# Row dots alternate with all searches but the first, in a two-layer decoder with a retrieval expert mixer

## The chip, the cores and the metric

The kernel runs on one core of one Trainium2 chip. The metric is device time in microseconds (us) of one execution. Before the change it was 1746.57 us, the median of 3 runs (1742.76 to 1748.43).

## The reference, cut to what matters

Two layers. Each has a mixer (attention in layer 0, a gated recurrence in layer 1) and then an expert channel mixer ("peer"). For every token and each of 8 heads the expert mixer scores two lists of 128 keys, takes the 16 best of each, adds them to 256 candidates, and keeps the 16 best. Each kept pair (i, j) names one of 16384 experts, with a row of 1024 numbers in table U and one in table V:

```python
sv, si = lax.top_k(s, PEER_TOPK)
cand = (sv[:, :, 0, :, None] + sv[:, :, 1, None, :]).reshape(-1, PEER_HEADS, PEER_TOPK * PEER_TOPK)
cidx = (si[:, :, 0, :, None] * N_KEYS + si[:, :, 1, None, :]).reshape(...)
top_s, top_p = lax.top_k(cand, PEER_TOPK)
eidx = jnp.take_along_axis(cidx, top_p, axis=-1)
g = jax.nn.softmax(top_s, axis=-1)
u = u_tab[eidx]
act = jax.nn.gelu(jnp.einsum('thkd,td->thk', u, xb).astype(jnp.float32))
w = (g * act).astype(xb.dtype)
return jnp.einsum('thk,thkd->td', w, v_tab[eidx])
```

There are 256 tokens and 16 meta tokens, 1024 channels, all in float32. Layer 0 mixes 272 tokens, layer 1 only 256.

## The kernel before, in words

The expert mixer (`peer`, once for each layer) handles its tokens in two ways.

The **dense** tokens, 160 in either layer, are multiplied with the whole of U and then the whole of V. Both tables stream through four buffers (`raw`), 128 tiles of 512 KB each, loaded by the SyncE queue (`load_read`): a buffer is loaded again when TensorE has used its tile. TensorE makes 8 float32 matmuls for a tile, which the trace records as 16. For the 160 tokens, the weights g are spread over the expert grid with one-hot matmuls (`hots` on VectorE, `products` on TensorE, `gate_act` on VectorE), in 20 groups of 8 tokens for each half of the grid. The groups of half 0 go between the last 40 tiles of U, two tiles to a group, those of half 1 between the first 40 tiles of V.

The **gathered** tokens, 112 in layer 0 and 96 in layer 1, only fetch the rows that they need. A "row" n is one gather by GpSimd of 128 U rows (then V rows) of 4 KB each, one for each partition, into one of 8 buffers (`bufs`), 512 KB in all. There are ROWS of them for U and as many for V: 112 + 112 in layer 0, 96 + 96 in layer 1. GpSimd fetches row n when its indices are found and row n - 8 has been used (`rows_taken`). VectorE uses a U row by a `dot` (L1482) with a copy of the tokens (`reps`), and a V row by `add_row` (L1496, L1499), a multiply-add into `reps`. Between the two stands `weigh_rows` (L1488), which waits for `row_gelus`: ScalarE's gelu over all dots (L1413). ScalarE's program has that gelu after its last U tile (`take_act`, L1396).

VectorE's program is written out in one order, and rows are dealt into it by hand. Positions of tiles below are counted in the U table or the V table, from 0 to 127.

1. `find`, the search over the score groups, two at a time: 17 groups in layer 0 (9 searches), 16 in layer 1 (8 searches). The first 7 groups (6 in layer 1) belong to gathered tokens. They come first and give the row indices. After each search with `first >= GG`, five in either layer, 6 dots follow (ROWS_PER_FIND).
2. Gates are shifted for the softmax, then 9 dots, then a wait for ScalarE's exp (L1404), which ScalarE makes after U tile 71. VectorE goes on at L1532.
3. The spread operands (`placed`), then 9 dots. TensorE needs `placed` at U tile 84 (L1633), and VectorE then waits for its result (L1548).
4. For half 0 and then half 1, 20 groups m: 2 rows, `gate_act` (L1307) of group m, `hots` (L1285 to L1292) of group m + 1. TensorE starts `products` (L1272) of a group when its `hots` are made, and V's first product (L1313) waits for all `gate_act` of half 0.
5. What is left: row k of `left` waits for V tile 40 + k * 78 // left.

```python
left = 2 * ROWS - n
for k in range(left):
    tile = NG * 2 + k * (LAST_ROW_TILE - NG * 2) // left
```

6. TensorE sums the gathered tokens' results (the folds, L1669) before V tile 112 (those of copies 0 to 2 in layer 0, 0 and 1 in layer 1) and the last copy before V tile 124. Folds 0 to 2 of layer 0 need 96 of its 112 V rows.

Of the kernel before, what the change touches and what calls it, by code (L numbers as in the profile page):

```python
# [35 lines left out]
PH, NK, TOPK, QH = 8, 128, 16, 128  # L36
# [1107 lines left out]
def peer(nc, ctx, mem, d, layer):  # L1144

    def sem(name):
        return ctx.sem(f"peer{layer}_{name}")
# [7 lines left out]
    GG, COPIES, TB = GH + EXTRA, GB + EXTRA, TD + GB * LANES  # L1155
# [68 lines left out]
    spaced, turned, reps_out = sem("spaced"), sem("turned"), sem("reps_out")  # L1224
# [13 lines left out]
    def copy_of(n):  # L1238

        return n // TOPK % GB if n < GH * TOPK else GB  # L1240
# [16 lines left out]
    def fold_at(b):  # L1257

        bank, at = (TURN_BANK, b) if b < 2 else (0, b - 2)
        _, width = tokens_of(b)  # L1260
        at = at * DC * LANES
        return mem.ps[:, bank, at:at + DC * width].rearrange("p (c t) -> p c t", t=width)
# [61 lines left out]
    with nc.Block() as block:  # L1324
# [94 lines left out]
        def _(dve):  # L1419
# [55 lines left out]
            def wait_row(n):  # L1475
                dve.wait_ge(row_in[n % NBUF], 16 * (n // NBUF + 1))

            def dot(n):

                wait_row(n)  # L1480
                buf = bufs[:, n % NBUF, :]
                dve.tensor_tensor_reduce(buf, buf, reps[:, copy_of(n), :], 1.0, 0.0, ALU.mult, ALU.add,  # L1482
                                         dots[:, n:n + 1]).then_inc(rows_taken, 1)
# [18 lines left out]
            def rows(first, last):  # L1502

                for n in range(first, min(last, 2 * ROWS)):
                    if n == ROWS:
                        weigh_rows()
                    if n < ROWS:
                        dot(n)
                    else:
                        add_row(n)  # L1510
                return min(last, 2 * ROWS)

            n = 0
            for first in range(0, G, 2):
                find(first, min(2, G - first))
                if first >= GG:
                    n = rows(n, n + ROWS_PER_FIND)
            step.wait(1)

# [10 lines left out]
            n = rows(n, n + ROWS_AT_SPREAD)  # L1530
# [12 lines left out]
            n = rows(n, n + ROWS_AT_SPREAD)  # L1543
# [7 lines left out]
            for half in range(2):  # L1551
# [3 lines left out]
                for m in range(NG):  # L1555
                    n = rows(n, n + ROWS_PER_GROUP[half])
# [4 lines left out]
            for k in range(left):  # L1561
                tile = NG * 2 + k * (LAST_ROW_TILE - NG * 2) // left
                dve.wait_ge(st.done, V0 * HALVES + 2 * tile)
                n = rows(n, n + 1)
# [236 lines left out]
```

## Time and profile before

| | |
|---|---|
| median of the runs | 1746.57 us |
| the profiled execution's own time | 1746.25 us |
| its span in the trace | 1744.5 us |
| TensorE matmuls busy | 95% |
| VectorE / GpSimd / ScalarE busy | 66% / 36% / 16% |
| moved by DMA | 533.94 MB, 306 GB/s over the span |
| of it the gathers' queue / the stream's queue | 218.13 MB / 314.90 MB |

The layers' expert mixers fill about 165 to 900 us and 1029 to 1735 us of the span. TensorE is busy nearly everywhere, but its busy time is no measure of how fast it goes through tiles: when a tile's data come late, the gap is short and comes often. So the stages are read by the time for one tile, the DMA rate and the granted clock.

### The profile page before, as it was taken

The page shows a single profiled execution, that of the slowest core. Times are in us where ns is not written, and L with a number is a line of the kernel's source. Part 1 is how long each engine was busy: PE and PEld are TensorE (multiplying, and loading weights), DVE is VectorE, ACT ScalarE, POOL GpSimd, SP SyncE. Part 2 cuts the span into 40 slices and gives each one's busy share as a digit, 9 for nine tenths or more (in the row PEclk, how much of TensorE's full clock was granted, in tenths as well). Part 3 has the DMA queues.
Part 4 walks back from the last instruction along what each step waited for, and adds up shares of the span by engine and source line. Part 5 has one row for each costly group of instructions (what it writes and reads, how often), then busy time and mean ns, then how long its engine had stood idle before and what let it go on. Part 6 is the DMA issues. An engine that isn't in the chain of part 4 may idle for free. (4 is left out here: it accounts for less than half of the span.)

```text
span 1744.5 us, 35217 instructions
## 1 busy us (share of the span) xinstructions
PE 1653.8 (95%) x12806; PEld 1550.5 (89%) x12806; DVE 1147.7 (66%) x2449; ACT 278.8 (16%) x752; POOL 631.6 (36%) x538
## 2 busy tenths in 40 slices
PE   8999999999999999999888999989999999999998
PEld 7858899888999998888778888988899999989897
DVE  4562369984699896545648823999458999944442
ACT  4553221111110000000025621211111100000000
POOL 5614011353244445333416621033433444533310
PEclk9999999999999999999899999999999999999999
DMA  4303477999999999999963235799999999999984
GB/s 155 133 13 102 133 265 270 364 381 366 344 408 403 389 398 408 410 409 410 394 241 112 97 125 178 258 349 354 392 336 354 408 391 395 409 405 403 383 341 157
DMA packets 149917, 533.94 MB, mean 306 GB/s; under 512 B 17617, under 2 KB 20434, under 8 KB 149842
## 3 DMA queue, kind: packets, MB, share of 16 engines
q1 hardware_dynamic: 89938, 314.90, 48.3%
q0 software_dynamic: 59904, 218.13, 32.4%
q8 instruction: 35, 0.57, 0.1%
q14 instruction: 40, 0.33, 0.1%
HBM read 531.92 MB, written 1.05 MB: 306 GB/s over the span
## 5 line engine op out<-in xcount | busy, mean ns | idle before, releaser
L308 PE MATMUL ps<-big,raw 128*128 128x160 f32 (+2 forms) x4608 | 701.3, 311 | 22.7 <-DMA raw<-in_u 16.9
L308 PEld LDWEIGHTS ps<-big,raw 128*128 128x128 f32 x4608 | 656.1, 190 | 55.5 <-issue 20.8
L1313 PE MATMUL ps<-big,raw 128*128 (+1 forms) x4096 | 600.9, 304 | 21.9 <-DMA raw<-in_v_rows 8.7
L1313 PEld LDWEIGHTS ps<-big,raw 128*128 128x128 f32 x4096 | 563.9, 191 | 49.6 <-issue 46.0
L1356 POOL DMA_INDIRECT big<-in_u_rows,big x208 | 252.8, 1215 | 589.4 <-DVE big L1482 414.6
L1499 DVE SCALAR_TENSOR_TENSOR big<-big 128x1024 f32<-128x1024 f32 x201 | 258.1, 1284 | 202.3 <-PE ps L1313 127.5
L1356 POOL DMA_INDIRECT big<-in_v_rows,big x208 | 225.8, 1086 | 314.2 <-DVE big L1499 255.9
L1482 DVE CUSTOM_DVE_ANT_0 big<-big 128x1024 f32<-128x1024 f32 x208 | 244.5, 1224 | 10.1 <-DMA big<-in_u_rows,big 10.1
L265 POOL TENSOR_TENSOR wlo<-raw,whi 128x512 fp32r<-128x512 f32 x98 | 136.6, 1411 | 94.5 <-ACT whi L259 94.1
L1396 ACT ACTIVATE big<-ps 128x160 f32 x256 | 77.6, 303 | 545.4 <-PE ps L308 510.7
L393 ACT ACTIVATE big<-h 128x272 f32<-128x272 f32 (+1 forms) x32 | 12.6, 418 | 585.5 <-DVE h L1573 575.2
L1430 DVE MAX8 big<-big 128x8 f32<-128x128 f32 (+1 forms) x99 | 33.6, 339 | 104.6 <-ACT big L1365 92.6
L292 PE MATMUL ps<-xhi,whi 128*128 128x272 f32 x312 | 88.7, 309 | 11.1 <-DVE xlo L432 9.5
L1292 DVE TENSOR_TENSOR i_gate<-i_hot,g 128x512 bf16<-128x512 bf16 x240 | 87.4, 422 | 0.0
L1307 DVE TENSOR_TENSOR big<-big,ps 128x512 f32<-128x512 f32 x80 | 55.0, 687 | 46.4 <-PE ps L1272 30.0
L293 PE MATMUL ps<-xlo,whi 128*128 128x272 f32 x312 | 85.0, 297 | 0.0
L292 PEld LDWEIGHTS ps<-xhi,whi 128*128 128x128 f32 x312 | 61.7, 198 | 15.2 <-issue 12.3
L1272 PEld LDWEIGHTS ps<-i_gate,j_hot 128*128 128x128 bf16 x1920 | 68.2, 97 | 5.5 <-DVE i_gate L1292 2.3
L1272 PE MATMUL ps<-i_gate,j_hot 128*128 128x64 bf16 x1920 | 71.1, 193 | 1.6 <-DVE i_gate L1292 1.6
L259 ACT CAST whi<-raw 128x512 fp32r<-128x512 f32 x98 | 58.6, 618 | 60.8 <-PE ps L297 50.4
L293 PEld LDWEIGHTS ps<-xlo,whi 128*128 128x128 f32 x312 | 61.8, 198 | 0.3
L1288 DVE TENSOR_TENSOR j_hot<-iota,idx 128x1024 bf16<-128x1024 bf16 x80 | 55.1, 689 | 0.0
(184 smaller groups left out, 1143.1 us busy)
## 6 DMA issues: line engine op xcount, KB each, us to landing
raw<-in_u SPq DMA_DIRECT2D x256, 512.0 KB
raw<-in_v_rows SPq DMA_DIRECT2D x256, 512.0 KB
raw<-in_query SPq DMA_DIRECT2D x32, 512.0 KB, 3.3
raw<-in_lru_w SPq DMA_DIRECT2D x24, 512.0 KB, 3.2
raw<-in_mla_down SPq DMA_DIRECT2D x17, 512.0 KB, 3.4
raw<-in_mla_out SPq DMA_DIRECT2D x8, 512.0 KB, 3.3
big<-in_u_rows,big POOLq DMA_INDIRECT x208
big<-in_v_rows,big POOLq DMA_INDIRECT x208
```

What stands on the lines that cost most here:

```text
L259: act.copy(self.mem.whi[:, q % SLOTS, :], self.mem.raw[:, s, e * HW:(e + 1) * HW]).then_inc(self.hi_ready, 1)
L265: eng.tensor_tensor(self.mem.wlo[:, q % SLOTS, :], self.mem.raw[:, s, e * HW:(e + 1) * HW], self.mem.whi[:, q % SLOTS, :].bitcast(F32), AL ...
L292: pe.matmul(out, w, m.xhi[:, x, 0:self.T], start=(x == 0), stop=False)
L293: pe.matmul(out, w, m.xlo[:, x, 0:self.T], start=False, stop=False)
L308: mm = pe.matmul(out, self.mem.raw[:, s, c * P:(c + 1) * P], x[:, c, :], start=(c == 0), stop=(c == DC - 1))
L1272: mm = pe.matmul(o, mem.j_hot[:, t // 2, :, t % 2], mem.i_gate[:, k, t // 2, :, t % 2], start=(k == 0), stop=(k == PARTS - 1))
L1292: ins = dve.tensor_tensor(mem.i_gate[:, k], mem.i_hot[:, :, :, :], pairs(mem.g[:, k, tok], wide_i), ALU.mult)
L1313: return pe.matmul(accumulator(c), mem.raw[:, s, c * P:(c + 1) * P], act_w[:, i, :], start=start, stop=False, skip_group_check=True)
L1356: pool.indirect_dma_start(bufs[:, b, :], None, (u_rows if n < ROWS else v_rows)[:, :], bass.IndirectOffsetOnAxis(rows_at[:, k:k + 1], 0)). ...
L1396: act.activation(act_w[:, bass.ds((turn - U0) * UNROLL + s, 1), :], mem.ps[:, s % 2, 0:TD].unsqueeze(1), ACT.Gelu_apprx_tanh).then_inc(st. ...
L1482: dve.tensor_tensor_reduce(buf, buf, reps[:, copy_of(n), :], 1.0, 0.0, ALU.mult, ALU.add, dots[:, n:n + 1]).then_inc(rows_taken, 1)
L1499: dve.scalar_tensor_tensor(rep, bufs[:, n % NBUF, :], w, rep, ALU.mult, ALU.add).then_inc(rows_taken, 1)
```

## The change

The condition after a search becomes `if first:`. The dots start after the second search: 8 times 6 in layer 0, 7 times 6 in layer 1. As dots now run before all copies of the tokens must have been made, the first dot of every 16 rows gets a wait for its copy.

```diff
             def dot(n):
 
                 wait_row(n)
+                if n % TOPK == 0:
+                    dve.wait_ge(reps_out, 2 * copy_of(n) + 2)
                 buf = bufs[:, n % NBUF, :]
                 dve.tensor_tensor_reduce(buf, buf, reps[:, copy_of(n), :], 1.0, 0.0, ALU.mult, ALU.add,
                                          dots[:, n:n + 1]).then_inc(rows_taken, 1)
...
             n = 0
             for first in range(0, G, 2):
                 find(first, min(2, G - first))
-                if first >= GG:
+                if first:
                     n = rows(n, n + ROWS_PER_FIND)
             step.wait(1)
```

## Rows read from the trace of the kernel before

**Rows 1.** Windows by stage: window, length, busy time (instructions) by engine, clock, DMA share, GB/s.
```profile
660.50:845.70 185.20, 174.38 (x1157) 158.36 (x1154) 97.94 (x78) 0.00 (x0) 77.07 (x77) 1.00 1.03 409
845.70:890.10 44.40, 36.54 (x242) 35.47 (x241) 25.81 (x22) 0.00 (x0) 14.95 (x13) 0.85 0.97 367
1517.50:1691.60 174.10, 167.01 (x1159) 157.70 (x1155) 77.40 (x62) 0.00 (x0) 57.18 (x58) 1.00 1.01 397
236.70:292.00 55.30, 55.30 (x410) 55.30 (x409) 52.17 (x201) 9.55 (x29) 0.00 (x0) 1.00 0.69 228
292.00:437.40 145.40, 136.42 (x939) 128.17 (x939) 112.35 (x309) 20.67 (x62) 62.10 (x48) 1.00 0.97 367
1137.00:1295.60 158.60, 149.19 (x1040) 141.85 (x1039) 118.04 (x333) 22.79 (x69) 63.85 (x48) 1.00 0.94 355
```

**Rows 2.** TensorE's waits: who waited for whom, us in total, times, longest.
```profile
PE ps L308 <- DMA raw<-in_u: 16.9, 34, 2.2
PE ps L1669 <- DVE big L1499: 6.6, 1, 6.6
```

**Rows 3.** Timeline of TensorE at the folds: start, length, instructions, idle before and releaser.
```profile
845.70 3.65 PE L1669 MATMUL ps<-con,big 128*128 128x32 f32 x32
855.99 3.62 PE L1669 MATMUL ps<-con,big 128*128 128x32 f32 x16 [6.64 <-DVE big L1499]
...
1695.13 26.33 PE L1313 MATMUL ps<-big,raw 128*128 128x160 f32 x192
```

**Rows 4.** Windows behind layer 0's fold (the clock stands before the DMA share).
```profile
856.00:860.00 4.00, 4.00 (x18) 4.00 (x19) 3.26 (x3) 0.00 (x0) 3.08 (x4) 0.50 1.04 410
860.00:865.00 5.00, 5.00 (x24) 5.00 (x23) 4.55 (x4) 0.00 (x0) 2.15 (x3) 0.60 1.00 392
```

**Rows 5.** Timeline of TensorE in layer 0's U tiles, between searches.
```profile
307.55 4.93 PE L308 MATMUL ps<-big,raw 128*128 128x160 f32 x32 [0.16 <-DMA raw<-in_u]
...
369.67 7.49 PE L308 MATMUL ps<-big,raw 128*128 128x160 f32 x48 [0.73 <-DMA raw<-in_u]
```

**Rows 6.** Timeline of VectorE from the searches to the spread, both layers.
```profile
246.19 0.19 DVE L1470 SCALAR_TENSOR_TENSOR big<-big 128x32 uint32<-128x32 f32 x1
...
290.20 1.22 DVE L1482 CUSTOM_DVE_ANT_0 big<-big 128x1024 f32<-128x1024 f32 x1
...
410.72 0.44 DVE L1532 TENSOR_REDUCE big<-big 128x17 f32<-128x272 f32 x1 [14.55 <-ACT big L1404]
...
438.83 0.56 DVE L1548 CAST idx<-ps 128x160 bf16<-128x160 f32 x2 [10.70 <-PE ps L1633]
...
1271.23 0.42 DVE L1532 TENSOR_REDUCE big<-big 128x16 f32<-128x256 f32 x1 [24.82 <-ACT big L1404]
```

**Rows 7.** Timeline of three engines where layer 1 goes from U to V.
```profile
1407.63 0.69 DVE L1307 TENSOR_TENSOR big<-big,ps 128x512 f32<-128x512 f32 x1
...
1410.17 1.23 DVE L1482 CUSTOM_DVE_ANT_0 big<-big 128x1024 f32<-128x1024 f32 x1
1411.28 0.89 PE L1272 MATMUL ps<-i_gate,j_hot 128*128 128x64 bf16 x24
...
1411.32 1.23 DVE L1482 CUSTOM_DVE_ANT_0 big<-big 128x1024 f32<-128x1024 f32 x1
1411.58 0.30 ACT L1396 ACTIVATE big<-ps 128x160 f32 x1 [1.87 <-PE ps L308]
...
1412.46 0.69 DVE L1307 TENSOR_TENSOR big<-big,ps 128x512 f32<-128x512 f32 x1
...
1413.40 3.77 PE L1313 MATMUL ps<-big,raw 128*128 128x160 f32 x26 [1.24 <-DVE big L1307]
```

**Rows 8.** Timeline of layer 0's gelu over dots and the first V rows.
```profile
619.98 0.30 ACT L1413 ACTIVATE big<-big 128x112 f32<-128x112 f32 x1 [66.13 <-DVE big L1482]
...
622.39 0.28 DVE L1488 TENSOR_TENSOR big<-big 128x112 f32<-128x112 f32 x1
...
623.58 1.28 DVE L1499 SCALAR_TENSOR_TENSOR big<-big 128x1024 f32<-128x1024 f32 x1
```

## The prediction

> **What bounds the kernel now.** I read the page's slices first, then TensorE's waits, then windows by stage, then timelines where two stages meet. TensorE is the path to the end, but three different things set its pace.
>
> In the first 25 tiles of layer 0's U table it sets its own pace: 410 matmul records are 25.6 tiles in 55.3 us, 2.16 us a tile, while DMA moves only 228 GB/s [rows 1]. At the end of layer 1, where no row is fetched any more, 12 tiles take 26.33 us, 2.19 us each [rows 3]. That is TensorE's own pace.
>
> From 292 to 437 us, where rows are fetched in bursts between searches, 939 records are 58.7 tiles in 145.4 us: 2.48 us a tile [rows 1]. The reader is to see the waits for in_u in many small pieces, 34 of them, none over 2.2 us [rows 2].
>
> In V behind the groups DMA is full. Layer 0: 72 tiles in 185.2 us, 2.57 us a tile, at 409 GB/s; layer 1: 72 tiles in 174.1 us, 2.42 us, at 397 GB/s [rows 1]. One transfer of 524 KB takes 1.28 us at 409 GB/s, and a tile and a row together 2.56 us. So layer 0's tail goes at one row for each tile, though 96 rows are dealt over 78 tiles (1.23 a tile): rows fall behind, and at the fold TensorE stands 6.64 us for them [rows 3], then works at half clock (0.50 and 0.60, so 1.2 GHz for most of 9 us) [rows 4]. Stretches differ in what a fetched row costs TensorE: nothing to 0.4 us early, and up to 1.28 us in a full tail.
>
> **The change, part by part.** Dots done at the end of the searches go from 30 to 48 in layer 0 and from 30 to 42 in layer 1. All later dealings keep their size, so every later row is 18 (12) earlier in VectorE's order, and `left` shrinks from 96 to 78 in layer 0 and from 64 to 52 in layer 1. The count of dots, gathers and bytes is the same. The first use of a buffer moves from behind the fifth search (dots at 290.20) to behind the second, whose indices are made at 246.19 [rows 6]; GpSimd's gathers follow, as each waits for the row 8 before it.
>
> *VectorE's chain* becomes later by 18 dots of 1.15 us (1410.17 to 1411.32 [rows 7]), 20.7 us, in layer 0 and by 13.8 us in layer 1. It now stands 14.55 and 24.82 us for ScalarE's exp, and in layer 0 again 10.70 us for TensorE's spread result [rows 6]. Layer 1 is covered. In layer 0 6 us are not, but the exp itself comes later by what TensorE loses below, and the second wait hides the rest. Were that cover gone, the price would be the difference, 6 us at most. I take 0.
>
> *The added wait* holds VectorE, and behind it the following searches, until a copy of the tokens is made. ScalarE makes all copies before the scores that the second search waits for, so it is over before it is reached. 0.
>
> *30 gathers move into early U tiles.* Before, three bursts of 6 stand between 307.55 and 369.67: 25 tiles in 62.1 us [rows 5] against 25 x 2.19 = 54.8, so 7.4 us for 18 gathers, 0.41 us each. Over 292 to 437.4: 145.4 - 58.7 x 2.19 = 16.8 us for 48 gathers, 0.35 each; layer 1, 1137 to 1295.6: 158.6 - 65 x 2.19 = 16.3 us for 48, 0.34 each [rows 1]. I take 0.38: +6.8 us in layer 0 (three bursts more), +4.6 us in layer 1 (two more). Bounds: 0, as DMA has 409 - 228 = 181 GB/s spare there [rows 1], and 1.28 each, 38 us, if nothing is spare. The rows nearest are the bursts themselves.
>
> The Trainium skill (DMA: Bandwidth & Descriptors, Queues, rings and completion order) says each DMA engine takes turns between its queue rows packet by packet. Layer 0's tail agrees (one row for one tile at 2.57 us a tile), and it speaks against this change: a burst of gathers takes half of the bandwidth while it lasts, however much is spare on average, and the tail's pace does not rise while a row is due for each tile.
>
> *Layer 0's tail.* 78 rows over 78 tiles is still one row for each tile, so tiles 40 to 110 stay at 2.56 us. Only the last two before the fold are free of gathers: -1 us. Between the bounds 0 and 185.2 - 72 x 2.19 = -27.5 I take this by the pair's own rate.
>
> *Layer 0's fold.* Row 208, the last that folds 0 to 2 need, is now due at tile 102, so the fold at tile 112 waits for nothing, and the last gathers are issued by tile 110. Before, 845.7 to 890.1 took 44.4 us [rows 1]. After: three folds at 3.65 / 2 = 1.83 us [rows 3], 5.5 us, and 12 tiles at 2.19, 26.3 us, together 31.8: -12.6 us. That holds the wait, the half clock and the late gathers.
>
> *Layer 1's tail.* 52 rows over 78 tiles are 0.67 a tile. With the tile that is 1.67 x 1.28 = 2.13 us of DMA for 2.19 us of TensorE: TensorE's pace again, with DMA nearly full. Before, 0.82 a tile made 2.33 us and 2.42 were measured. I take 2.25: 162 us for 174.1, -12 us. Bounds: 0, and 174.1 - 157.7 = -16.4.
>
> *A new wait in layer 1.* U rows there are 96. Before, 48 + 40 dots are done when half 0 of the groups ends, and row 96 comes in half 1. After, 42 + 18 + 2 x 18 = 96: row 96, and with it `weigh_rows`, stands at group 18 of half 0, ahead of `gate_act` of group 18 and `hots` of group 19. It waits for a gelu that ScalarE makes only after the last U tile. It is no deadlock, as TensorE can do both last tiles without `hots` of group 19, but then TensorE stands. By rows: ScalarE takes the last tile from 1411.58 to 1411.88 [rows 7]; gelu 0.30, to 1412.2; weigh and first V row 1.19 (622.39 to 623.58), second 1.28 [rows 8], to 1414.7; gate_act and hots 2.54 (1407.63 to 1410.17), to 1417.2, where products were at 1411.28. Then two more rows, 2.57, to 1419.8, and V starts 0.94 after the gate_act (1412.46 to 1413.40), at 1420.7 for 1413.40 [rows 7]: +7.3 us. TensorE has then stood some 5.8 us, and after 6.64 us it fell to 1.2 GHz, which cost half of 4 us and 2 of the next 5 [rows 3, 4]; part falls in the wait here, so +3.2. Together +10.5. Bounds: 0 if hidden, 14 with twice the clock loss. Layer 0 has 112 U rows: 48 + 18 + 40 = 106, so its row 112 falls into half 1, where the gelu is free. 0.
>
> **The sum.** +6.8 + 4.6 - 1 - 12.6 - 12 + 10.5 = -3.7 us on the profiled execution's own 1746.25: 1742.5. That execution is 0.3 us under the median of the runs, so 1743 against 1746.57.
>
> **The rivals.**
> (A) *Layer 1's new wait doesn't cost.* For it: V behind it waits for data in small pieces (2.42 us a tile against 2.19), and four filled buffers could give some back. Against: the groups' stretch behind it is TensorE's, and its own tail has little left to give. Without +10.5: 1732.
> (B) *Layer 0's tail speeds up.* If arbitration favours the stream once fewer rows are outstanding, tiles go at 2.40, not 2.57: -12 more, 1731. Against: 2.57 us a tile holds for 72 tiles on end.
> (C) *Slower, by the early bursts.* They now start at tile 5, and layer 0 has eight in a row, so buffers never refill. The highest price of a burst is the 0.41; if it is 0.8 for each of 30 gathers, they cost 24 for 11.4, and the sum is +8.9: 1755.5. From 0.68 on the change is slower by the bound below. For it: in 292 to 437 DMA is at 0.97 with only 367 GB/s. Against: two layers give 0.34 and 0.35.
> (D) *Layer 1's tail stays at 2.42 us a tile*, since its irregular dealing, and not bytes, makes its gaps: +12, 1755.
> (E) *The dots don't run early*, since a row or copy is late. The rows were long there when the first dot ran at 290.20 [rows 6]: no wait of VectorE for DMA stands ahead of it. 1746.5.
>
> **How the numbers follow.** About 5 us (0.3%) either way is what runs of this kernel can tell from no change. Forecast 0.50 (own range 1737 to 1750; 0.12 of it below 1741.3, 0.36 same, 0.02 slower), A 0.15, B 0.08, C 0.14, D 0.10, E 0.03. Faster 0.12 + 0.15 + 0.08 = 0.35; same 0.36 + 0.03 and 0.01 of C's near end: 0.40; slower 0.25. Range 1730 to 1757.
>
> **What would show it.** First dot near 246 us, bursts of 6 from 248 on, U tile 84 of layer 0 near 444 instead of 437. No wait of TensorE at layer 0's fold, its clock 1.00 there; 2.56 us a tile before, 2.19 after. In layer 1 weigh_rows (L1488) ahead of the last `products` of half 0, with TensorE idle near 6 us and a clock under 1.00. A tail of layer 1 near 162 us. I am wrong if the early U tiles lose much more or less than 11 us, if the new wait is missing, or if either tail goes at another pace.

## The result

Over 20 executions of each kernel the median went from 1748.60 to 1756.37 us: ratio 1.0048, 95% interval 1.0029 to 1.0067. The change makes the kernel 0.5% slower; 1743 us was forecast for it, with "no change" as the likeliest outcome. One of the changed kernel's 20 executions took 3346.73 us and is not in the ratio.

The profile after needs care. Its execution took 1745.20 us (span 1743.4), the least of the 20 and 1 us less than the profiled execution before. The two spans say nothing about the change; the stages do. Windows of the changed kernel, to be read beside [rows 1] (length, busy time and instructions by engine, clock, DMA share, GB/s):

```profile
663.70:848.10 184.40, 174.52 (x1159) 158.41 (x1155) 92.19 (x73) 0.00 (x0) 71.82 (x72) 1.00 1.03 409
848.10:881.20 33.10, 33.10 (x242) 33.10 (x242) 8.37 (x8) 0.00 (x0) 0.00 (x0) 0.95 0.64 219
1521.20:1690.60 169.40, 162.53 (x1157) 157.26 (x1154) 62.12 (x50) 0.00 (x0) 44.23 (x46) 1.00 0.98 370
232.80:441.40 208.60, 194.75 (x1347) 183.79 (x1346) 185.42 (x545) 30.35 (x91) 81.56 (x66) 1.00 0.95 360
1083.30:1289.70 206.40, 193.84 (x1347) 183.68 (x1346) 171.43 (x508) 30.28 (x91) 77.56 (x60) 1.00 0.94 353
```

The five windows are layer 0's tail and fold, layer 1's tail, and the first 84 U tiles of either layer. Fold of layer 0: 44.4 us became 33.1, with no gather left in it. Tail of layer 0: 184.4 for 185.2, at the same 409 GB/s. Tail of layer 1: 169.4 for 174.1, with 12 gathers less but DMA at 0.98 and only 370 GB/s. The first 84 U tiles, the same 1347 matmul records, take 208.6 and 206.4 us. Over the same tiles the kernel before took 200.7 (236.7 to 437.4) and 200.1 us (1095.5 to 1295.6), with 48 gathers in each for 66 and 60 now. TensorE's waits (us in total, times, longest), beside [rows 2]:

```profile
PE ps L308 <- DMA raw<-in_u: 23.8, 51, 1.6
PE ps L1272 <- DVE i_gate L1292: 6.6, 3, 5.7
```

The wait of the fold (L1669, 6.64 us) is gone; 51 small waits for U tiles stand for 34, and a new one of 5.7 us for `hots`. Here it is, where layer 1 goes from U to V, beside [rows 7] and [rows 8] (timeline):

```profile
1405.38 0.30 ACT L1396 ACTIVATE big<-ps 128x160 f32 x1 [1.87 <-PE ps L308]
1405.58 0.27 ACT L1413 ACTIVATE big<-big 128x96 f32<-128x96 f32 x1
...
1405.88 0.26 DVE L1490 TENSOR_TENSOR big<-big 128x96 f32<-128x96 f32 x1 [7.01 <-ACT big L1413]
1406.18 0.75 DVE L1498 TENSOR_SCALAR big<-big 128x1024 f32<-128x1024 f32 x1
1407.05 1.28 DVE L1501 SCALAR_TENSOR_TENSOR big<-big 128x1024 f32<-128x1024 f32 x1
...
1408.25 0.68 DVE L1307 TENSOR_TENSOR big<-big,ps 128x512 f32<-128x512 f32 x1
...
1410.79 2.67 DVE L1501 SCALAR_TENSOR_TENSOR big<-big 128x1024 f32<-128x1024 f32 x2
1410.93 1.46 PE L1272 MATMUL ps<-i_gate,j_hot 128*128 128x64 bf16 x24 [5.69 <-DVE i_gate L1292]
...
1414.31 1.14 PE L1313 MATMUL ps<-big,raw 128*128 128x160 f32 x3 [1.92 <-DVE big L1307]
```

`weigh_rows` (now L1490) stands 7.01 us for ScalarE's gelu over the dots, which comes only behind the last U tile; the V rows (L1498, L1501), the gate (L1307) and the `hots` queue behind it, and TensorE's `products` wait 5.69 us for those. Behind this idle time the granted clock stands at 0.50, that is 1.2 GHz, for two windows of 5 us:

```profile
1405.00:1410.00 5.00, 0.24 (x2) 0.00 (x0) 3.96 (x7) 1.76 (x3) 1.99 (x2) 0.97 0.63 200
1410.00:1415.00 5.00, 2.15 (x27) 2.03 (x28) 4.90 (x9) 0.00 (x0) 2.53 (x3) 0.50 0.67 206
1415.00:1420.00 5.00, 5.00 (x20) 5.00 (x20) 3.47 (x5) 0.00 (x0) 2.53 (x3) 0.50 0.66 206
```

Why the span hides the loss is outside the changed stages. In attention, where both kernels are the same, the execution before ran a while at half clock and the one after did not (windows of before, then of after):

```profile
130.00:135.00 5.00, 5.00 (x18) 3.88 (x17) 0.00 (x0) 2.79 (x7) 1.41 (x2) 0.50 0.00 0
```
```profile
130.00:135.00 5.00, 5.00 (x37) 4.66 (x37) 0.44 (x1) 3.31 (x6) 3.10 (x4) 1.00 0.02 3
```

Layer 0's U tiles begin 3.9 us earlier after it (232.8 for 236.7), and between the end of layer 0 and layer 1's U tiles, before the first early dot of layer 1, another 3.2 us are gained: 7.1 us that the change didn't bring. That the clock makes most of the 3.9 us fits the other profiles: thirteen (all but e10's) have the same code up to layer 0's U tiles, which begin anywhere from 232.8 to 238.8 us, and in the five with a mean clock of 0.66 from 125 to 140 us they begin at 236.3 us or later.

### The profile page after: what moved, and what is told of

Same layout as the page of the kernel before. It is cut to its first block and busy times, and to the rows that moved or that the text cites. A ratio compares the mean times of both kernels' runs of the same rounds, so it can differ in the third digit from the quotient of the medians.

```text
span 1743.4 us, 35228 instructions
## 1 busy us (share of the span) xinstructions
PE 1649.6 (95%) x12806; PEld 1546.6 (89%) x12806; DVE 1148.1 (66%) x2449; ACT 278.6 (16%) x752; POOL 638.6 (37%) x538
## 5 line engine op out<-in xcount | busy, mean ns | idle before, releaser
L1501 DVE SCALAR_TENSOR_TENSOR big<-big 128x1024 f32<-128x1024 f32 x201 | 257.8, 1283 | 217.1 <-PE ps L1313 191.4
L1356 POOL DMA_INDIRECT big<-in_v_rows,big x208 | 234.6, 1128 | 349.9 <-DVE big L1501 282.0
L393 ACT ACTIVATE big<-h 128x272 f32<-128x272 f32 (+1 forms) x32 | 12.6, 418 | 648.0 <-DVE h L1575 637.8
L1307 DVE TENSOR_TENSOR big<-big,ps 128x512 f32<-128x512 f32 x80 | 54.7, 683 | 43.1 <-PE ps L1272 26.2
```

The lines of the kernel that those rows point to most:

```text
L1356: pool.indirect_dma_start(bufs[:, b, :], None, (u_rows if n < ROWS else v_rows)[:, :], bass.IndirectOffsetOnAxis(rows_at[:, k:k + 1], 0)). ...
L1501: dve.scalar_tensor_tensor(rep, bufs[:, n % NBUF, :], w, rep, ALU.mult, ALU.add).then_inc(rows_taken, 1)
```

## The experiments

Twelve kernels ran, in three groups; in each group the kernel before ran beside them on the same chip, and its medians there are 1738.14 (e0 to e3), 1737.47 (e4, e5, e7, e8) and 1740.11 us (e6, e9, e10, e12). e5, e6, e8, e9 and e10 ran once each, so they are read by their stages alone. Stages are lengths between TensorE's rows in the profiles: "U" is U tiles 0 to 83, "end of U" tiles 84 to 127, "V start" V tiles 0 to 39, "tail" V tiles 40 to 111, "fold" from the first fold (L1669) to the last.

**The change again, whole and by layer.** e0_after_again is the changed kernel unaltered. The other two:

```diff
-                if first:
+                if first >= (2 if layer == 0 else GG):    # e2_layer0_only
+                if first >= (2 if layer == 1 else GG):    # e3_layer1_only
```

> The changed kernel unaltered, once more, to see which of its stages repeat. Theory 1 (the stages of the expert mixers make the change: by the first profile +7.8 early and -11.3 at the fold in layer 0, +6.2, +6.8, +2.8 and -4.7 in layer 1, together about +6 us): those stages repeat within 1.5 us, and the time is 4 to 9 us above the kernel before. Rival (the whole difference is drift between executions, since the first profile of the changed kernel was even 1 us shorter than the one before): the stages spread by more than 3 us and the time is within 3 us of the kernel before.

> Early dots in layer 0 alone, layer 1 as before. Theory 1: layer 0 pays 7.8 us early and gets 0.9 + 0.9 + 11.3 back in its tail and at its fold, so 5 us under the kernel before. Rival (the changes of layer 0 cancel, its fold wait being worth less in most executions than in the one profiled): within 2 us of the kernel before.

> Early dots in layer 1 alone, layer 0 as before. Theory 1: 6.2 + 6.8 + 2.8 - 4.7 = 11 us above the kernel before. The prediction's sizes would give 4.6 + 10.5 - 12 = +3. Rival (cancelling in layer 0, above): about +8, the whole difference.

Measured ratios to the kernel before: e0 1.0059 (1.0040 to 1.0078), +10.2 us; e2 0.9986 (0.9970 to 1.0003), -2.4 us; e3 1.0078 (1.0058 to 1.0098), +13.6 us. The two parts add up to 11.2. The loss is layer 1's. Layer 0's gain is not resolved from none. A layer that a kernel leaves alone serves as another profile of before, so each stage has two profiles unchanged and three changed (means, us):

| stage | layer 0 | | | layer 1 | | |
|---|---|---|---|---|---|---|
| | unchanged | changed | difference | unchanged | changed | difference |
| U | 199.5 | 208.5 | +9.0 | 199.3 | 205.7 | +6.4 |
| end of U | 117.4 | 117.5 | +0.1 | 117.3 | 123.9 | +6.6 |
| V start | 104.4 | 103.9 | -0.5 | 104.0 | 106.6 | +2.6 |
| tail | 185.1 | 184.5 | -0.6 | 174.2 | 171.5 | -2.7 |
| fold | 44.2 | 33.1 | -11.1 | 29.7 | 30.8 | +1.1 |
| sum | | | -3.1 | | | +14.0 |

The sums agree with the measured -2.4 and +13.6 us. Stages with the same code spread by up to 5 us among these five profiles, most in layer 1's tail (169.4, 170.9, 174.2), so a single profile would not have shown this. The later kernels e1, e4, e5, e6, e8 and e9 leave all of layer 0, and the U tiles 0 to 83 of layer 1, as in the changed kernel. With them nine profiles stand for either: layer 0's U is 205.9 us in the mean (202.0 to 209.6) and layer 1's 206.0 (203.8 to 207.4), so +6.4 and +6.7 us against the two unchanged ones. The +9.0 of the table comes from three profiles that happened to be long. e3 also shows the fold wait where layer 0 is unchanged (timeline), so it was no accident of the first profile:

```profile
852.68 3.62 PE L1671 MATMUL ps<-con,big 128*128 128x32 f32 x16 [6.56 <-DVE big L1501]
```

**Layer 1's new wait taken away.** e1_cap_half0:

```diff
-                    n = rows(n, n + ROWS_PER_GROUP[half])
+                    n = rows(n, min(n + ROWS_PER_GROUP[half], ROWS if half == 0 else 2 * ROWS))
```

> Rows of half 0 of the groups stop at the last U row, so that weigh_rows never stands in half 0. Theory 1 (the new wait in layer 1 costs its 7 us and 3 us of half clock): the last 44 U tiles of layer 1 fall from 124.6 to 118 us, the first 40 V tiles from 106.9 to 104, and 4 more rows in the tail cost about 1 us: 8 to 9 us under the changed kernel, 0 to 3 us under the kernel before. Rival (stalls there are given back, as full buffers follow them): under 4 us gained.

Ratio 1.0001 (0.9983 to 1.0019), 10 us under e0 (1.0059). End of U 115.8 us, V start 103.8, no wait at V's first product beyond the usual:

```profile
1402.12 4.58 PE L1313 MATMUL ps<-big,raw 128*128 128x160 f32 x32 [0.98 <-DVE big L1307]
```

So the wait costs what the stages say, and no later stage gives a visible part of it back; its tail, with 56 rows, took 175.9 us. This one wait is the whole difference between the changed kernel and the one before, as far as the interval of about 3 us either way can tell: without it, the rest of the change comes out at nothing.

**How much of it is the clock.** e4_filler is the changed kernel with the last turn of layer 1's U tiles written out:

```diff
+                    if s == GROUPS_AFTER[1]:
+                        keep_busy(pe, mem, TURN_BANK, 44)
                     if s in GROUPS_AFTER:
                         products(pe, 0, NG - 2 + GROUPS_AFTER.index(s))
+                keep_busy(pe, mem, TURN_BANK, 12)
```

> The changed kernel with filler matmuls in layer 1 where TensorE waits (44 before the last products of half 0, 12 behind them), so that it stays active; the waits themselves stay. Theory 1 (the fall to 1.2 GHz is what costs the stage behind the wait its 2.8 us and the products 0.6): granted clock 1.00 there, the first 40 V tiles of layer 1 from 106.5 to 104 us, the last 44 U tiles 123 to 124 us as before, 3 us under the changed kernel. Rival (the slow tiles behind the wait come from late data, not from the clock): 106 us stay.

Ratio 1.0032 (1.0009 to 1.0055), 4.7 us under e0 with intervals that overlap. Timeline and one window:

```profile
1399.15 4.97 PE L202 MATMUL ps<-filler 128*128 128x256 bf16 x44
1405.00 0.90 PE L1272 MATMUL ps<-i_gate,j_hot 128*128 128x64 bf16 x24 [0.89 <-DVE i_gate L1292]
...
1408.38 4.59 PE L1313 MATMUL ps<-big,raw 128*128 128x160 f32 x32 [1.17 <-DVE big L1307]
```
```profile
1410.00:1415.00 5.00, 5.00 (x57) 4.96 (x57) 3.82 (x6) 0.00 (x0) 2.36 (x2) 1.00 0.85 288
```

The clock stays at 1.00 and V start falls to 104.0 us, while the end of U stays at 123.7. So 2.6 us of the two stages' 9.2 are the half clock, the rest is the wait. This rests on the stages; the total alone would not show it.

**What a fetched row costs where DMA has room.** The prediction had layer 1's tail near 162 us. These leave out V rows of layer 1's tail (n is cut at 2 * ROWS - SKIP in GpSimd's and VectorE's loops and in the folds' waits); e9 deals its rows in pairs. A row that is left out is neither fetched by GpSimd nor added by VectorE:

```diff
+    SKIP = 52 if layer == 1 else 0        # e5; 13 in e8, 26 in e6 and e9
-            for n in range(2 * ROWS):
+            for n in range(2 * ROWS - SKIP):
...
+                kk = k - k % 2 if layer == 1 else k        # e9
+                tile = NG * 2 + kk * (LAST_ROW_TILE - NG * 2) // left
```

> The changed kernel without the last 52 V rows of layer 1: they are neither fetched nor added (part of the computation is left out). Its tail (V tiles 40 to 111) is then stream alone. The prediction's threshold and the rival price agree here: 72 tiles at TensorE's own 2.19 us, 158 us, for 169 to 171 with the rows.

> The changed kernel with only 39 of the last 52 V rows of layer 1, dealt evenly, one row every second tile (13 rows are left out of the computation). DMA is asked for 1.5 transfers for each tile, 1.92 us of DMA for 2.19 us of TensorE. Theory T (the prediction's: a row costs nothing while DMA has room): 158 to 160 us for V tiles 40 to 111. Theory P (a fixed price for each row): about 158 + 39 x 0.24 = 167. Theory I (irregular dealing makes the gaps, not the number): 158 to 160, and 26 rows dealt in pairs would be dearer than 26 dealt singly.

> The changed kernel with only 26 of the last 52 V rows of layer 1, one every third tile (26 rows are left out of the computation). So far V tiles 40 to 111 of layer 1 took 156.6 us with no row, 170.2 with 39 and 169.4 to 170.9 with 52. Price for each row (0.35 us): 165 to 167 us. Threshold further down (DMA asked for 1.33 transfers a tile): 157 to 159.

> The same 26 rows, dealt in pairs, two every sixth tile. If a row costs because it lengthens the landing of the three loads under way, two at once lengthen it more but half as often: within 3 us of single dealing. If unevenness is what costs, over 5 us more than single dealing.

| rows in layer 1's tail | 0 | 26 | 26 in pairs | 39 | 52 | 56 | 64 |
|---|---|---|---|---|---|---|---|
| tail, us | 156.6 | 167.6 | 167.2 | 170.2 | 169.4, 170.9, 173.7, 174.2 | 174.1, 175.9 | 174.1, 174.3, 177.6 |
| us a row over 156.6 | | 0.42 | 0.41 | 0.35 | 0.30 | 0.33 | 0.29 |

The columns of 52, 56 and 64 rows hold every profile with that number (173.7 is e4, 174.1 with 56 rows e7, 177.6 e12); the last row goes by their means.

With no rows all of it is one unbroken stretch:

```profile
1520.96 156.74 PE L1314 MATMUL ps<-big,raw 128*128 x1152
```

No threshold shows down to 26 rows: these already cost 11 us, at one third of a row for a tile, and the step from 64 to 52 rows is worth some 3. Regular dealing doesn't help (39 rows) and pairs don't harm. The DMA view (window of 100 us; issues, KB, median us from issue to landing) says why. For e5, e8 and e1 in layer 1's tail, then e0 among the U tiles of layer 1:

```profile
raw<-in_v_rows SPq DMA_DIRECT2D x46, 512.0 KB, 3.7
```
```profile
raw<-in_v_rows SPq DMA_DIRECT2D x42, 512.0 KB, 6.2
big<-in_v_rows,big POOLq DMA_INDIRECT x22, 7.3
```
```profile
raw<-in_v_rows SPq DMA_DIRECT2D x41, 512.0 KB, 6.3
```
```profile
raw<-in_u SPq DMA_DIRECT2D x36, 512.0 KB, 6.6
```

A buffer is reloaded when its tile is used, and it is needed again three tiles later, after 3 x 2.19 = 6.6 us. Alone, loads land in 3.7 us. In e8, with one row for two tiles, a gather takes 7.3 us to land, so one is nearly always under way, and the median load lands in 6.2 us, though DMA carries only 331 GB/s in that window. The traces hold the landings of only some of the loads. The quickest, the median and the slowest of them, for the loads of e5 and then e8 in the same windows, and what TensorE waited for in the whole tail of e8 (in e5's it waited for nothing):

```profile
DMA to landing us min/median/max: 3.1/3.7/4.8
```
```profile
DMA to landing us min/median/max: 3.5/6.2/7.2
```
```profile
PE ps L1314 <- DMA raw<-in_v_rows: 9.0, 11, 1.6
```

So without rows no load comes near 6.6 us, and with them the slowest come after it; the waits that this view counts are 9.0 of the 13.6 us. The pairs of e9 show it tile by tile: every six tiles two gathers go out, and TensorE then does six tiles (96 records) without a break and waits once for a load:

```profile
1555.10 13.30 PE L1314 MATMUL ps<-big,raw 128*128 x96 [0.98 <-DMA raw<-in_v_rows]
1569.53 13.30 PE L1314 MATMUL ps<-big,raw 128*128 x96 [1.13 <-DMA raw<-in_v_rows]
```

The median of its recorded loads is 4.6 us, under the lead: only loads beside a pair come late, and a median doesn't show them. What TensorE waits for is a load each time, never VectorE, so it is the gathers that cost and not the adding that was left out with them.

**The lead made shorter.** e10_short_lead:

```diff
     def load_read(self, sp, turn, s, src):
-        sp.wait_ge(self.done, (turn - 1) * HALVES + 2 * (s + 1))
+        sp.wait_ge(self.done, (turn - 1) * HALVES + 2 * (s + 1) + 1)
```

> The changed kernel with every load of the stream in the expert mixers issued half a tile later (it waits until TensorE has also used the first half of the next tile). Nothing else changes. A buffer is free for 3 tiles (6.6 us at TensorE's pace) before it is needed; the load lands after 3.7 us with no rows and after 6.2 to 6.6 us (median) with rows beside it. Theory L (rows cost by making the landing longer than this lead): with 2.5 tiles, 5.5 us, nothing changes where no rows are fetched (12 tiles behind the fold of layer 1, 29.7 us), while the U tiles between searches and layer 1's tail lose 8 us or more each (layer 0's U stage from 207 to over 215, layer 1's tail from 170 to over 178). Rival (rows cost through the DMA rate alone, which is full at moments): those stages stay within 3 us.

1832.79 us. Windows of layer 0's U tiles and of layer 1's tail, and the 12 tiles behind layer 1's fold on the timeline:

```profile
237.40:462.20 224.80, 195.94 (x1347) 185.39 (x1346) 184.90 (x545) 30.33 (x91) 89.00 (x66) 0.99 0.91 341
1593.50:1777.50 184.00, 165.11 (x1159) 157.47 (x1156) 61.94 (x50) 0.00 (x0) 44.95 (x46) 1.00 0.93 340
```
```profile
1781.02 26.33 PE L1313 MATMUL ps<-big,raw 128*128 128x160 f32 x192
```

Where rows are fetched, the same tiles take 15 us or more longer in layer 0's U (224.8, for 202.0 to 209.6 over nine profiles) and 9 to 14 us longer in layer 1's tail (183.4, as 0.6 of the 184.0 stand before tile 40, for 169.4 to 174.2), while DMA is less busy than in the first profile after (0.91 for 0.95, 0.93 for 0.98). Where none are, nothing changes (26.33 us, as in [rows 3]). What rows cost hangs on the lead of the loads. That more lead, with more than the four buffers, would make rows free was not tried.

**Bursts or single gathers.** e7_spread_dots, on top of e1:

```diff
-                find(first, min(2, G - first))
-                if first:
-                    n = rows(n, n + ROWS_PER_FIND)
+                def one():
+                    nonlocal n
+                    n = rows(n, n + 1)
+                find(first, min(2, G - first), one if first > 2 else None)
+                if first == G - (2 - G % 2):
+                    n = rows(n, n + ROWS_PER_FIND)
```

`find` calls `one` after three of the five steps of each of its two top-16 searches.

> As e1_cap_half0, but the six dots are spread through the next search, one after every second or third step of it, instead of in a row after it, so that gathers leave one by one, about 3.5 us apart. Same rows, same bytes. Theory B (it is the burst that costs, since six gathers in a row take half of the bandwidth for 15 us and three loads ahead can't cover that): the first 84 U tiles fall from 202 to 207 us to under 196 in both layers, so 10 to 20 us under e1_cap_half0. Theory P (every gather delays a tile by 0.35 to 0.5 us wherever it stands): 202 to 207 us stay, time within 3 us of e1_cap_half0.

Ratio 0.9961 (0.9941 to 0.9980); U 205.2 us in layer 0 and 201.1 in layer 1. Layer 1's U is 5 us under the 206.7 of e1 and under all nine profiles with bursts (203.8 or more); layer 0's is 3 us over its 202.1 but inside the stage's spread. Neither theory's number is met: U doesn't fall below 196, and against e1 the kernel gains 7 us by the ratios (0.9961 for 1.0001), with intervals that just miss each other, or 4.6 by the medians, and not the 10 to 20 of theory B nor the 3 at most of theory P. That bursts cost more than single gathers is so in layer 1 and open in layer 0.

**A version from the runs.** e12_more_in_layer0, e7 with:

```diff
-                find(first, min(2, G - first), one if first > 2 else None)
+                find(first, min(2, G - first), one if first > (2 if layer == 0 else GG) else None)
+                if layer == 0 and first:
+                    one()
```

> A version by what the runs show: rows of half 0 stop at the last U row; in layer 0 one dot more at each search (8 more, all spread through the searches), so that its tail gets 72 rows for 78 tiles, under one a tile; in layer 1 the dots start at the old place, but spread through the searches. Expected against e7_spread_dots: layer 0 early +3 us, its tail 184 to about 177 us, layer 1 within 2 us; against the kernel before 0.6% less time (e7 0.4% less). Rival: the tail of layer 0 stays at 184 us, as near the full rate a row fewer buys nothing; then equal to e7 or 3 us slower.

Ratio 0.9917 (0.9888 to 0.9946), median 1725.09 us: it beats both kernels. Windows of layer 0's U tiles and tail, then layer 1's:

```profile
237.70:440.90 203.20, 193.32 (x1347) 183.72 (x1346) 188.09 (x550) 30.24 (x91) 87.14 (x67) 1.00 0.97 372
664.00:845.70 181.70, 171.69 (x1156) 158.08 (x1153) 85.97 (x69) 0.00 (x0) 65.75 (x66) 1.00 1.02 401
1081.30:1276.70 195.40, 189.34 (x1347) 183.25 (x1346) 157.27 (x480) 30.19 (x91) 62.80 (x48) 1.00 0.92 343
1497.60:1675.10 177.50, 168.67 (x1156) 157.81 (x1153) 76.78 (x62) 0.00 (x0) 58.36 (x58) 1.00 1.00 387
```

Layer 0 has 74 dots done before its groups, for 66 in the changed kernel. Its U tiles take 203.2 us, within the 202.0 to 209.6 of the changed kernel's, and its fold takes 33.1 us without a wait. Its tail of 72 rows is 181.7, not the 177 expected. Layer 1 with its 30 dots spread has U at 195.4 for 199.3, but its tail of 64 rows is 177.6 for 174.2. All stages of the table together make -10 us against the unchanged ones, and the profiled execution, 1729.76 us, is 10.4 us under the kernel before. The rest of the 14 us lies between this execution and the median, 4.7 us below it.

## Why the prediction was wrong

- **Layer 1's tail was the step that failed.** The prediction put 52 rows at 2.25 us a tile, 162 us, "TensorE's pace again": -12 us. Measured: 171.5 for 174.2, -2.7 (-2.1 with e4's tail). The rule behind it, that a row costs nothing while DMA has room on average, is false here: 26 rows cost 11 us (e6), and the price is there from the lowest number tried, as it works through the landing time against a lead of three tiles (e5, e8, e10). The prediction's own early rows, 0.34 to 0.41 us each at DMA shares under 1, contradicted the tail's price of near zero (0.06 us a tile over 2.19, so 4 us for 52 rows); it used one price early and another late for the same thing. Its own check of the rule on the tail before had come out short too: 2.33 us a tile by the rule, 2.42 measured. Its rival D had nearly the outcome (+12) but gave irregular dealing as the cause; e8, dealt regularly, pays 0.35 us a row all the same.
- **Early gathers** were right in layer 0 and undersized in layer 1: over nine profiles +6.4 and +6.7 us for 6.8 and 4.6, 0.44 us each for 30 instead of 0.38 (the table's three profiles give +9.0 and +6.4, 0.51 each). The mechanism and place held; rival C's price of 0.8 did not.
- **The new wait of layer 1** was right in place, order and size: +6.6 and +2.6 us for 7.3 and 3.2, and e1 gives 10 us for the 10.5. That the clock would fall was right too (e4).
- **Layer 0's fold** -11.1 for -12.6; **its tail** -0.6 for -1, still at one row a tile and 409 GB/s.
- **VectorE's chain** stayed hidden, as forecast: the wait for the exp shrank from 14.55 to 0.88 us in layer 0 and from 24.82 to 14.72 in layer 1, and the second wait of layer 0 from 10.70 to 7.63:

```profile
413.03 0.44 DVE L1534 TENSOR_REDUCE big<-big 128x17 f32<-128x272 f32 x1 [0.88 <-ACT big L1404]
...
442.81 0.55 DVE L1550 CAST idx<-ps 128x160 bf16<-128x160 f32 x2 [7.63 <-PE ps L1635]
...
1263.18 0.42 DVE L1534 TENSOR_REDUCE big<-big 128x16 f32<-128x256 f32 x1 [14.72 <-ACT big L1404]
```

- **The sum.** From -3.7: tail of layer 1 +9.3, early gathers +4.0, the smaller terms +1.3, which makes +10.9, for +8.4 measured first and +10.2 with e0; with the nine profiles' U it is +8.6. Costs of 21.9 us, half of them the wait, against gains of 25.6 us made a near zero sum, and half of those gains rested on one assumption. The tail's term alone turns the sum from -3.7 to +5.6. Seeing the wait was worth more than the sum: it alone decides the sign.

## What to carry to other kernels

In this kernel the stream of tiles paid for the rows fetched beside it wherever its slowest loads landed later than their lead (three free buffers times the time for one tile, 6.6 us), though DMA moved only 331 GB/s. So compare the landing time under load, of the slowest loads too, with the lead, and not only GB/s with the most that was seen. And when work is dealt into an engine's program by count, moving the count moves the point at which a dependency falls due: look for what stands at that point before and after.

## What the runs showed of the hardware that was not expected

- One gather of 512 KB for two tile loads of 512 KB, evenly spaced, lengthened the loads' median landing from 3.7 to 6.2 us (e5, e8, of the loads whose landing the trace holds), with DMA at 319 to 360 GB/s while rows were fetched, below the 409 that other stretches reach.
- Half a tile less lead (1.1 us) on loads cost some 86 us over the kernel, 5% (e10 beside e0's median, one execution).
- The same code in attention ran at clock 0.50 in one profile and at 1.00 in another. The start of layer 0's U tiles moved by up to 6 us (232.8 to 238.8) between thirteen profiles of code that is the same up to there; the executions of one kernel, where 12 or more were timed, spread over 10 to 24 us.
